# Hybrid attention and mLSTM trunk on one core: f32r scores of split keys and queries, queries moved among the value products, gated outputs a head sooner, roots by Ln and Exp

## The chip, the cores and the metric

One NeuronCore of a Trainium2 chip runs the whole program, with no other core at work. The metric is the device time of one execution in microseconds, as the median over runs. All times in the text are microseconds unless another unit stands beside them.

## What the kernel computes

The reference is a causal trunk of two layers over 512 tokens of 1024 features. Each layer is a half-step SwiGLU FFN, a token mixer and a second half-step FFN. The first layer mixes by dilated attention and pooling; the second by an mLSTM block. The change sits almost wholly in the mLSTM block, cut here to what matters (four heads of 512 channels, `x_c` the convolved tokens, `x_m` the unconvolved ones):

```python
x_m, z = split(xn @ w_in)
x_c = silu(conv(x_m) + conv_b)
q, k, v = blockdiag(x_c, wq), blockdiag(x_c, wk), blockdiag(x_m, wv)   # blocks of 4 channels
...
s_qk = einsum('bhte,bhse->bhts', q, k) * exp(dm - m_t)                 # causal
num, den = s_qk @ v, sum(s_qk)
hh = rms_norm(num / max(abs(den), exp(-m_t)), out_gain)
y = (hh + skip * x_c) * silu(z)
return y @ w_out
```

The kernel does not step through chunks; it takes all 512 tokens of a head at once. The norms before every FFN and mixer are `x * rsqrt(mean(x*x) + 1e-6)`.

## The kernel before

The order of work is written out by hand: each engine has its own list of instructions, and semaphores join them. Data lie features in front of tokens. Most products are taken in float32r, as three products of operands split into a high part (a copy rounded to float32r, written by ScalarE) and a low part (operand less high part, written by VectorE): high by high, low by high, high by low. A few small products are taken in plain float32.

The mLSTM block of `odd_mixer` first runs the input projection, then the four heads, then the output projection (`Q_OOUT`). One head h, on TensorE, before the change:

- **A** (`joined`): the product of the block-diagonal query and key weights, four 128x128 tiles in plain float32. Its input BD is built by GpSimd (`block_diagonals`), and ScalarE copies its result to AM.
- **q0 to q3** (`query`): AM by `x_c`, 512 wide, plain float32; ScalarE copies each to Q.
- **v0 to v3** (`value`): plain float32; ScalarE makes VH of each, then VectorE makes VL.
- **M, EM** (`row`): rows broadcast over the partitions, f32r.
- **mean square** (`mean_square(h - 1)`): sums over the channels the squares of the head before.
- **s0 to s3** (`score`): keys by queries for key block j, 512, 384, 256 and 128 tokens wide, four plain float32 products each.
- **products** j = 0 to 3: the weighted scores by the values, into banks 0 to 3, and the denominator into bank 4. Split on both sides: 12 f32r products and 2 for the denominator each.

A, q, v, M, EM and s are "items". Items go round three PSUM banks (5, 6, 7) in the order of TensorE's list, so item r has to wait until item r - 3 has been read:

```python
if r >= 3:
    pe.wait_ge(item_read[r % 3], r // 3)
return PS[5 + r % 3]
```

What is read: q by ScalarE (L1411), v by ScalarE (VH, L1469) and then VectorE (VL, L2108), s by VectorE (`weighted`, L2118). The chain from a score to the products is: ScalarE takes the weight by Exp (`weight`, L1474), GpSimd cuts it to the causal part (`causal`, L2327), VectorE multiplies the score in (`weighted`), ScalarE takes the high part PTH (`product_high`, L1479), VectorE the low part PTL (`weighted_low`, L2122), TensorE multiplies by the values.

The output of a head runs behind, during the next heads: four squares of the numerator on ScalarE (L1459), which read banks 0 to 3 after the last product; their three sums on VectorE (`squares`, L2073), where the fourth square waits for the first sum since it reuses SQX; the mean square on TensorE; `head_factor` on VectorE; the square root on ScalarE (L1452); its reciprocal on VectorE (`invert_factor`, L2091); `scale_numerator` and `add_skip` on VectorE; `gated` (times silu(z)) on GpSimd; YH on ScalarE and YL (`y_low`, L2322) on GpSimd. The gated outputs of head h - 2 are made during head h.

The ring of four slots that holds the projections' weights (raw, then high and low part) has free places during the heads: slot 3 holds VL, and slots 0 to 2 receive the first three weight tiles of the output projection.

## Time and profile before

| what | value |
|---|---|
| median of 3 runs | 1954.96 us (1954.4 to 1955.63) |
| the profiled execution's own time | 1955.77 us |
| its span in the trace | 1954.0 us |
| PE busy, share of the span | 100% |
| DVE, ACT, POOL busy | 72%, 44%, 27% |
| TensorE's granted clock | 9 (of tenths) in all 40 slices |
| the four heads, first query to the output projection | 1411.66 to 1517.98 us |

The profile is of one execution. A row of a timeline gives the start, the time taken, the engine, the source line and the operation, and behind it in brackets the engine's idle time before it and who ended it. PE's rows overlap, because matmuls are pipelined: what a matmul costs TensorE is the distance from its start to the start of the next, and not the time in its row. A plain float32 matmul leaves two records, so a row of 8 of them is four matmuls.

### The profile page before, as it was taken

Reading aid. Unit: us, or ns where it says so; the run is one execution under the profiler, and the core shown is the slowest. Engines: PE = TensorE matmul, PEld = TensorE weight load, DVE = VectorE, ACT = ScalarE, POOL = GpSimd, SP = SyncE. Lnnn points to the kernel's source line nnn. Section 1 sums busy time; section 2 is a strip of 40 time slices with the busy share of each in tenths; the row PEclk is TensorE's granted clock in tenths of the full one; section 3 lists DMA queues with packets and bytes.
Section 4 is the critical chain, followed back from the end, with each engine's and each line's share of the span. In section 5 each row is a group of like instructions: output and inputs, shape, how many; then the busy total and the mean of one; then the engine's idle time right before and its main releaser. Section 6 shows DMA issues by size and latency. Waiting matters only on the chain.

```text
span 1954.0 us, 28996 instructions
## 1 busy us (share of the span) xinstructions
PE 1948.1 (100%) x11722; PEld 1707.3 (87%) x11722; DVE 1397.9 (72%) x1882; ACT 851.6 (44%) x1230; POOL 527.3 (27%) x394
## 2 busy tenths in 40 slices
PE   9999999999999999999999999999999999999999
PEld 7999998877789999988999998877777888999997
DVE  7877776554588877768877776773458657877773
ACT  6443333535554344345433444442546345333431
POOL 1322222142223322223322322200015413322221
PEclk9999999999999999999999999999999999999999
DMA  6556663351346666545666653232200235666653
GB/s 211 155 164 171 173 168 95 119 181 55 88 126 176 174 172 167 147 129 145 178 166 172 181 151 114 97 96 88 76 1 1 87 116 160 177 173 168 178 141 107
DMA packets 112469, 265.92 MB, mean 136 GB/s; under 512 B 10321, under 2 KB 22865, under 8 KB 112337
## 3 DMA queue, kind: packets, MB, share of 16 engines
q1 hardware_dynamic: 92336, 225.72, 35.3%
q0 software_dynamic: 19856, 38.28, 12.5%
q8 instruction: 93, 1.52, 0.3%
q14 instruction: 40, 0.32, 0.0%
q10 hardware_dynamic: 144, 0.09, 0.0%
HBM read 259.32 MB, written 4.72 MB: 135 GB/s over the span
## 4 chain that ended last, share of the span: by engine, by line
PE 98%; DVE 1%; DMA 0%; issue 0%; ACT 0%; SPq 0%; POOL 0%; DVEq 0%
PE BANKS L656 12%; PE BANKS L658 12%; PE BANKS L657 12%; PE BANKS L579 11%; PE BANKS L580 11%; PE BANKS L581 11%; PE BANKS L709 6%; PE BANKS L710 6%; PE BANKS L711 6%; PE BANKS L1022 2%; PE BANKS L850 1%; PE BANKS L852 1%; PE BANKS L851 1%; PE BANKS L999 1%; PE BANKS L1005 1%; PE BANKS L813 1%
## 5 line engine op out<-in xcount | busy, mean ns | idle before, releaser
L656 PE MATMUL BANKS<-BF,ASH 128*128 128x256 f32 x876 | 248.0, 283 | 0.0
L658 PE MATMUL BANKS<-BF,ASL 128*128 128x256 f32 x876 | 247.9, 283 | 0.0
L657 PE MATMUL BANKS<-BFL,ASH 128*128 128x256 f32 x876 | 247.9, 283 | 0.0
L579 PE MATMUL BANKS<-XH,HI 128*128 128x512 f32 x624 | 245.7, 394 | 0.7 <-DVE XL L1593 0.3
L1657 DVE TENSOR_TENSOR LO<-RING,HI 128x1024 fp32r<-128x1024 f32 (+2 forms) x204 | 216.3, 1060 | 41.2 <-ACT HI L1160 39.9
L580 PE MATMUL BANKS<-XL,HI 128*128 128x512 f32 x624 | 243.2, 390 | 0.0
L581 PE MATMUL BANKS<-XH,LO 128*128 128x512 f32 x624 | 243.0, 389 | 0.0
L1173 ACT ACTIVATE TMP<-TMP 128x512 f32<-128x512 f32 x88 | 55.7, 633 | 406.4 <-DVE TMP L1686 406.4
L2262 POOL TENSOR_TENSOR TMP<-TMP,RSTD 128x512 f32<-128x512 f32 x88 | 132.0, 1499 | 365.3 <-ACT TMP L1173 365.3
L2254 POOL DMA_DIRECT2D ASR<-gu_dram x73 | 88.1, 1219 | 387.5 <-DMA ASR<-gu_dram 381.5
L709 PE MATMUL BANKS<-HH,DHI 128*128 128x512 f32 x488 | 190.7, 391 | 0.0
L710 PE MATMUL BANKS<-HL,DHI 128*128 128x512 f32 x488 | 190.6, 391 | 0.0
L1160 ACT ACTIVATE HI<-RING 128x1024 fp32r<-128x1024 f32 (+2 forms) x204 | 171.4, 876 | 42.3 <-DMA RING<-down_dram 21.4
L711 PE MATMUL BANKS<-HH,DLO 128*128 128x512 f32 x488 | 189.8, 389 | 0.0
L1676 DVE TENSOR_TENSOR ASL<-ASR,ASH 128x1024 fp32r<-128x1024 f32 x146 | 181.6, 1246 | 0.0
L2264 POOL TENSOR_TENSOR HL<-TMP,HH 128x512 fp32r<-128x512 f32 x88 | 139.0, 1580 | 146.6 <-ACT HH L1179 146.6
L1584 DVE TENSOR_TENSOR LO<-RING,HI 128x1024 fp32r<-128x1024 f32 x66 | 85.3, 1294 | 121.6 <-ACT HI L1102 121.5
L656 PEld LDWEIGHTS BANKS<-BF,ASH 128*128 128x128 f32 x876 | 168.2, 192 | 0.0
L657 PEld LDWEIGHTS BANKS<-BFL,ASH 128*128 128x128 f32 x876 | 168.2, 192 | 0.0
L658 PEld LDWEIGHTS BANKS<-BF,ASL 128*128 128x128 f32 x876 | 168.2, 192 | 0.0
L658 PE MATMUL BANKS<-XH,LO 128*128 128x256 f32 x584 | 165.3, 283 | 0.0
L657 PE MATMUL BANKS<-XL,HI 128*128 128x256 f32 x584 | 165.2, 283 | 0.0
(249 smaller groups left out, 4875.5 us busy)
## 6 DMA issues: line engine op xcount, KB each, us to landing
RING<-gu_dram SPq DMA_DIRECT2D x174, 512.0 KB, 3.9
ASR<-gu_dram SPq DMA_DIRECT2D x146, 256.0 KB, 2.9
ASR<-gu_dram POOLq DMA_DIRECT2D x73, 512.0 KB, 6.9
DRAW<-down_dram SPq DMA_DIRECT2D x40, 512.0 KB, 3.7
RING<-oin_dram SPq DMA_DIRECT2D x32, 512.0 KB, 3.5
RING<-down_dram SPq DMA_DIRECT2D x32, 384.0 KB, 3.2
DRAW<-down_dram SPq DMA_DIRECT2D x24, 384.0 KB, 3.7
RING<-ein_dram SPq DMA_DIRECT2D x16, 512.0 KB, 3.6
```

The lines of the kernel that those rows point to most:

```text
L579: pe.matmul(PS[bank][:], HI[j][:, c], hi(k), start=(n == 0), stop=False)
L580: pe.matmul(PS[bank][:], HI[j][:, c], lo(k), start=False, stop=False)
L581: last = pe.matmul(PS[bank][:], LO[j][:, c], hi(k), start=False, stop=(n == len(order) - 1))
L656: pe.matmul(out, w_hi[:, c], x_hi(k), start=(k == 0), stop=False)
L657: pe.matmul(out, w_hi[:, c], x_lo(k), start=False, stop=False)
L658: last = pe.matmul(out, w_lo[:, c], x_hi(k), start=False, stop=(k == 3))
L709: pe.matmul(bank, DHI[:, col], HH[:, h % 8, :], start=(k == 0), stop=False)
L710: pe.matmul(bank, DHI[:, col], HL[:, h % 8, :], start=False, stop=False)
L711: last = pe.matmul(bank, DLO[:, col], HH[:, h % 8, :], start=False, stop=(h == tiles[-1]))
L1160: act.activation(HI[j][:, cols], RAW[j][:, cols], ACT.Copy).then_inc(hi_ready, 1)
L1657: dve.tensor_tensor(LO[j][:, cols], RAW[j][:, cols], HI[j][:, cols].bitcast(F32), ALU.subtract).then_inc(lo_ready, 1)
L1676: dve.tensor_tensor(ASL[:, p % 2, 2 * i:2 * i + 2, :], ASR[:, p % 2, 2 * i:2 * i + 2, :], ASH[:, p % 2, 2 * i:2 * i + 2, :].bitcast(F32), ...
```

## The change

Four things are done, in one diff.

1. **Scores.** ScalarE makes the high part of the keys (XCH, two instructions of 1024 columns a head) and of each query (QH), VectorE the low parts (XCL, QL), and the scores are twelve f32r products a key block where there were four plain float32 ones. Each query item is now read twice, by ScalarE and then by VectorE. XCH, XCL and QL lie in ring slots 0, 1 and 2, so the output projection's first three weight tiles are loaded only when the last score of the last head is done.
2. **Queries.** For heads 1 to 3 the item A stands after the products of j = 0 of the head before (it stood after j = 1), q0 and q1 after those of j = 1, and q2 and q3 after those of j = 2.
3. **Gated outputs.** `gated`, YH and YL of head h - 1 are made during head h, behind the block diagonals on GpSimd.
4. **Roots.** In `norm` and in `root`, Sqrt on ScalarE and reciprocal on VectorE become Ln and Exp (scale -0.5) on ScalarE. TensorE waits for the finished root where it waited for the Sqrt.

The diff, cut to its core:

```diff
 def head_order(h):
-    start = [("q", 0), ("q", 1), ("v", 0), ("q", 2), ("q", 3), ("M", 0), ("v", 1)]
...
-        middle = [("EM", 0), ("v", 2), ("s", 0), ("v", 3), ("s", 1)]
...
+        order = [("v", 0), ("M", 0), ("v", 1), ("v", 2), ("EM", 0), ("s", 0), ("v", 3), ("s", 1)]
...
+            items += [(h + 1, "A", 0)] + [(h + 1, "q", c) for c in range(HT_)]
...
+                    elif q0 == Q_OIN:
+                        sp.wait_ge(item_done, ITEM[(HC - 1, "s", TT - 1)] + 1)
...
                     for c in range(HT_):
-                        last = pe.matmul(ps[:, 0:T - P * j], XC[:, HT_ * h + c, j * P:j * P + P], Q[:, c, j * P:],
-                                         start=(c == 0), stop=(c == HT_ - 1))
+                        pe.matmul(out, XCH[:, c, keys], QH[:, c, j * P:], start=(c == 0), stop=False)
+                        pe.matmul(out, XCH[:, c, keys], QL[:, c, j * P:], start=False, stop=False)
+                        last = pe.matmul(out, XCL[:, c, keys], QH[:, c, j * P:], start=False, stop=(c == HT_ - 1))
...
-                        if j == 1 and h + 1 < HC:
+                        if j == 0 and h + 1 < HC:
                             joined(h + 1)
+                        elif j < TT - 1 and h + 1 < HC:
+                            if j == 1:
+                                read_out(pe, (h + 1, "A", 0))
+                            query(h + 1, 2 * j - 2)
+                            query(h + 1, 2 * j - 1)
...
-                act.activation(RSTD[:], AUX[:], ACT.Sqrt, scale=1.0 / DM, bias=EPST[:]).then_inc(std_ready, 1)
+                link(act.activation(RSTD[:], AUX[:], ACT.Ln, scale=1.0 / DM, bias=EPST[:]))
+                act.activation(RSTD[:], RSTD[:], ACT.Exp, scale=-0.5).then_inc(rstd_ready, 1)
...
+                    if h + 1 < HC:
+                        keys_high(h + 1)
+                        query_high(h + 1, 0)
+                        query_high(h + 1, 1)
+                        y_high(h - 1, 0)
+                        y_high(h - 1, 1)
+                        query_high(h + 1, 2)
+                        y_high(h - 1, 2)
+                        query_high(h + 1, 3)
+                        y_high(h - 1, 3)
+                    else:
+                        split_hi(Q_OOUT, 0, 8)
+                        split_hi(Q_OOUT, 1, 8)
+                        y_high(h - 1, 0)
+                        y_high(h - 1, 1)
+                        split_hi(Q_OOUT, 2, 8)
...
-                dve.wait_ge(std_ready, r + 1)
-                dve.reciprocal(RSTD[:], RSTD[:]).then_inc(rstd_ready, 1)
...
+                def next_head(h):
+                    if h < HC:
+                        keys_low(h, 0)
+                        query_low(h, 0)
+                        query_low(h, 1)
+                        keys_low(h, 2)
+                        query_low(h, 2)
+                        query_low(h, 3)
+                    else:
+                        for j in range(3):
+                            split_lo(Q_OOUT, j, 8)
```

How the instructions stand, at the three places that count. On TensorE, from the last product of a head (L1060, the denominator's last row) to the first score of the next (L1022; names: XC is `x_c`, XM is `x_m`, SELR with MEM are the rows M and EM, SQ the mean square), before:

```order
L1060 MATMUL BANKS<-PTL,SELR 128x128
L999 MATMUL BANKS<-XC,AM 128x512 x2
L1005 MATMUL BANKS<-BD,XM 128x128 x4
L999 MATMUL BANKS<-XC,AM 128x512 x2
L1014 MATMUL BANKS<-MEM,SELR 128x512
L1005 MATMUL BANKS<-BD,XM 128x128 x4
L994 MATMUL BANKS<-SQ,CST 128x512
L1014 MATMUL BANKS<-MEM,SELR 128x512
L1005 MATMUL BANKS<-BD,XM 128x128 x4
```

and the same place of the changed kernel, whose line for the last product is L1070:

```order
L1070 MATMUL BANKS<-PTL,SELR 128x128
L1011 MATMUL BANKS<-BD,XM 128x128 x4
L1020 MATMUL BANKS<-MEM,SELR 128x512
L1011 MATMUL BANKS<-BD,XM 128x128 x8
L1000 MATMUL BANKS<-SQ,CST 128x512
L1020 MATMUL BANKS<-MEM,SELR 128x512
```

The four queries are gone from here, and v1 and v2 follow each other directly ahead of the mean square.

On ScalarE, from the four squares (L1459) to the first two weights (L1474), before:

```order
L1459 ACTIVATE SQX<-BANKS 128x512
L1411 ACTIVATE Q<-BANKS 128x512 x2
L1469 ACTIVATE VH<-BANKS 128x512
L1464 ACTIVATE RSTD<-BANKS 128x512
L1411 ACTIVATE Q<-BANKS 128x512 x2
L1411 ACTIVATE TMP<-BANKS 128x512
L1469 ACTIVATE VH<-BANKS 128x512
L1452 ACT_TABLE_LOAD
L1452 ACTIVATE RSTD<-RSTD 128x512
```

and after the change, with the squares at L1491, VH at L1501 and the root at L1483 and L1484:

```order
L1491 ACTIVATE SQX<-BANKS 128x512
L1501 ACTIVATE VH<-BANKS 128x512
L1496 ACTIVATE RSTD<-BANKS 128x512
L1427 ACTIVATE TMP<-BANKS 128x512
L1501 ACTIVATE VH<-BANKS 128x512 x2
L1483 ACT_TABLE_LOAD
L1483 ACTIVATE RSTD<-RSTD 128x512
L1484 ACT_TABLE_LOAD
L1484 ACTIVATE RSTD<-RSTD 128x512
L1506 ACTIVATE TMP<-TMP,ACOL 128x512
```

VH of v0 stands directly behind the squares, VH of v2 ahead of the root, and the root is two activations with two table loads.

On GpSimd, a head that has an earlier head's output to make, before (L2327 is `causal`, L2317 `gated`, L2322 `y_low`, L2308 the block diagonals):

```order
L2317 TENSOR_TENSOR TMP<-TMP,SZ 128x512 x4
L2327 AFFINE_SELECT TMP<-TMP 128x128
L2322 TENSOR_TENSOR YL<-TMP,YH 128x512
L2327 AFFINE_SELECT TMP<-TMP 128x128
L2322 TENSOR_TENSOR YL<-TMP,YH 128x512
L2327 AFFINE_SELECT WT_96<-WT_96 128x128
L2322 TENSOR_TENSOR YL<-TMP,YH 128x512
L2327 AFFINE_SELECT TMP<-TMP 128x128
L2322 TENSOR_TENSOR YL<-TMP,YH 128x512
L2308 TENSOR_TENSOR BD<-W,CST 128x512 x3
```

and after:

```order
L2398 AFFINE_SELECT TMP<-TMP 128x128 x2
L2398 AFFINE_SELECT WT_99<-WT_99 128x128
L2398 AFFINE_SELECT TMP<-TMP 128x128
L2381 TENSOR_TENSOR BD<-W,CST 128x512 x3
L2388 TENSOR_TENSOR TMP<-TMP,SZ 128x512 x4
L2393 TENSOR_TENSOR YL<-TMP,YH 128x512 x4
```

The eight output instructions moved behind the block diagonals, in one piece.

## Rows read from the trace of the kernel before

**Rows 1.** The page: span, parts 1 and 4

```profile
span 1954.0 us, 28996 instructions
...
PE 98%; DVE 1%; DMA 0%; issue 0%; ACT 0%; SPq 0%; POOL 0%; DVEq 0%
```

**Rows 2.** Waits of TensorE: engine, line waited for: us, times, longest

```profile
PE BANKS L1022 <- DVE VL L2108: 0.4, 1, 0.4
```

**Rows 3.** Timeline of PE, third head: start us, us, engine, line, operation

```profile
1463.26 0.28 PE L1059 MATMUL BANKS<-PTH,SELR 128*128 128x256 f32 x1
1463.38 0.28 PE L1060 MATMUL BANKS<-PTL,SELR 128*128 128x256 f32 x1
...
1464.89 0.27 PE L1060 MATMUL BANKS<-PTL,SELR 128*128 128x128 f32 x1
1465.01 1.93 PE L999 MATMUL BANKS<-XC,AM 128*128 128x512 f32 x4
...
1470.54 1.02 PE L994 MATMUL BANKS<-SQ,CST 128*128 128x512 f32 x2
...
1471.63 1.05 PE L1005 MATMUL BANKS<-BD,XM 128*128 128x128 f32 x8
1472.52 3.60 PE L1022 MATMUL BANKS<-Q,XC 128*128 128x512 f32 x8
...
1476.85 5.36 PE L1022 MATMUL BANKS<-Q,XC 128*128 128x384 f32 x24
1481.96 0.47 PE L1052 MATMUL BANKS<-PTH,VH 128*128 128x512 f32 x1
1482.28 0.39 PE L1053 MATMUL BANKS<-PTL,VH 128*128 128x512 f32 x1
1482.50 0.40 PE L1054 MATMUL BANKS<-PTH,VL 128*128 128x512 f32 x1
```

**Rows 4.** Timeline of ACT, third head

```profile
1463.98 0.60 ACT L1459 ACTIVATE SQ<-BANKS 128x512 f32<-128x512 f32 x1 [1.34 <-PE BANKS L1054]
...
1465.88 0.60 ACT L1459 ACTIVATE SQX<-BANKS 128x512 f32<-128x512 f32 x1 [0.33 <-DVE SQ L2073]
...
1471.41 1.28 ACT L1452 ACT_TABLE_LOAD   x1
1472.82 0.63 ACT L1452 ACTIVATE RSTD<-RSTD 128x512 f32<-128x512 f32 x1
```

**Rows 5.** Timeline of DVE, third head

```profile
1466.69 0.69 DVE L2073 TENSOR_TENSOR SQ<-SQ,SQX 128x512 f32<-128x512 f32 x1
1468.57 0.69 DVE L2108 TENSOR_TENSOR VL<-BANKS,VH 128x512 fp32r<-128x512 f32 x1 [1.19 <-ACT VH L1469]
...
1474.65 3.34 DVE L2091 RECIPROCAL RSTD<-RSTD 128x512 f32<-128x512 f32 x1
...
1479.89 1.72 DVE L2122 TENSOR_TENSOR PTL<-TMP,PTH 128x512 fp32r<-128x512 f32 x1
```

**Rows 6.** Timeline of POOL, third head

```profile
1479.80 1.27 POOL L2322 TENSOR_TENSOR YL<-TMP,YH 128x512 fp32r<-128x512 f32 x1
1481.02 0.75 POOL L2327 TENSOR_SCALAR_AFFINE_SELECT TMP<-TMP 128x128 f32<-128x128 f32 x1
...
1482.98 3.90 POOL L2308 TENSOR_TENSOR BD<-W,CST 128x512 f32<-128x512 f32 x3
```

**Rows 7.** Groups of DVE by line and form: the norms' reciprocals

```profile
L1610 DVE RECIPROCAL RSTD<-RSTD 128x512 f32<-128x512 f32 x6 | 20.1, 3350 | 17.4 <-ACT RSTD L1123 17.4
```

**Rows 8.** Timeline of PE at the end of the heads

```profile
1517.98 0.45 PE L579 MATMUL BANKS<-YH,HI 128*128 128x512 f32 x1
```

**Rows 9.** Timeline of DVE at the end of the heads

```profile
1519.67 0.69 DVE L2073 TENSOR_TENSOR SQ<-SQ,SQX 128x512 f32<-128x512 f32 x1
```

**Rows 10.** The page, part 6: the projection's weights

```profile
RING<-oin_dram SPq DMA_DIRECT2D x32, 512.0 KB, 3.5
```

More of the change, by code:

```diff
@@ L132, in head_order @@
 def head_order(h):
-    start = [("q", 0), ("q", 1), ("v", 0), ("q", 2), ("q", 3), ("M", 0), ("v", 1)]
     if h == 0:
-        middle = [("v", 2), ("v", 3), ("EM", 0), ("s", 0), ("s", 1)]
-    else:
-        middle = [("EM", 0), ("v", 2), ("s", 0), ("v", 3), ("s", 1)]
-    return start + middle + [("s", 2), ("s", 3)]
+        order = [("q", 0), ("q", 1), ("v", 0), ("q", 2), ("q", 3), ("M", 0), ("v", 1), ("v", 2), ("v", 3), ("EM", 0),
+                 ("s", 0), ("s", 1)]
+    else:
+        order = [("v", 0), ("M", 0), ("v", 1), ("v", 2), ("EM", 0), ("s", 0), ("v", 3), ("s", 1)]
+    return order + [("s", 2), ("s", 3)]
 def core_items():
@@ L149, in core_items @@
         if h + 1 < HC:
-            items.append((h + 1, "A", 0))
+            items += [(h + 1, "A", 0)] + [(h + 1, "q", c) for c in range(HT_)]
     return {item: r for r, item in enumerate(items)}
@@ L1413, in read, with keys_high, query_high @@
                     return r
+                def keys_high(h):
+                    if h:
+                        act.wait_ge(item_done, ITEM[(h - 1, "s", TT - 1)] + 1)
+                    for n in range(0, HT_, 2):
+                        act.activation(XCH[:, n:n + 2, :], XC[:, HT_ * h + n:HT_ * h + n + 2, :],
+                                       ACT.Copy).then_inc(xch_ready, 1)
+                def query_high(h, c):
+                    r = ITEM[(h, "q", c)]
+                    act.wait_ge(item_done, r + 1)
+                    act.activation(QH[:, c, :], PS[5 + r % 3][:], ACT.Copy).then_inc(qh_ready, 1)
                 for lq in range(8):
@@ L1451, in root @@
                         act.wait_ge(factor_ready, h + 1)
-                        act.activation(RSTD[:], RSTD[:], ACT.Sqrt).then_inc(tstd_ready, 1)
+                        link(act.activation(RSTD[:], RSTD[:], ACT.Ln))
+                        act.activation(RSTD[:], RSTD[:], ACT.Exp, scale=-0.5).then_inc(factor_root, 1)
                 def square_numerator(h, c):
@@ L1483, in odd_mixer @@
                         square_numerator(h - 1, c)
-                    read(h, "q", 0, Q[:, 0, :])
-                    read(h, "q", 1, Q[:, 1, :])
-                    value_high(h, 0)
-                    denominator(h - 1)
-                    read(h, "q", 2, Q[:, 2, :])
-                    read(h, "q", 3, Q[:, 3, :])
-                    if h:
+                    if h == 0:
+                        query_high(h, 0)
+                        query_high(h, 1)
+                        value_high(h, 0)
+                        query_high(h, 2)
+                        query_high(h, 3)
+                    else:
+                        value_high(h, 0)
+                        denominator(h - 1)
                         read(h, "M", 0, TMP[:, 6, :])
@@ L1493, in odd_mixer @@
                     value_high(h, 1)
-                    root(h - 1)
                     value_high(h, 2)
@@ L2087, in head_factor, with root_ready @@
                                              ALU.add).then_inc(factor_ready, 1)
[L2089 to L2091 removed]
+                def root_ready(h):
+                    dve.wait_ge(factor_root, h + 1)
                 def scale_numerator(h, c):
@@ L2109, in value_low, with query_low @@
                                       ALU.subtract).then_inc(read, 1)
+                def query_low(h, c):
+                    ps, read = item(h, "q", c)
+                    dve.wait_ge(qh_ready, HT_ * h + c + 1)
+                    dve.tensor_tensor(QL[:, c, :], ps[:], QH[:, c, :].bitcast(F32), ALU.subtract).then_inc(read, 1)
                 def row_copy(h, name, n):
@@ L2123, in weighted_low @@
                                       ALU.subtract).then_inc(ptl_ready, 1)
+                def next_head(h):
[6 more added lines that the diff above has]
+                        query_low(h, 3)
+                    else:
+                        for j in range(3):
+                            split_lo(Q_OOUT, j, 8)
+                query_low(0, 0)
+                query_low(0, 1)
                 value_low(0, 0)
+                query_low(0, 2)
+                query_low(0, 3)
                 row_copy(0, "M", 6)
@@ L2156, in odd_mixer @@
                     weighted_low(h, 2)
+                    weighted(h, 3)
                     add_skip(h - 1, 2)
-                    weighted(h, 3)
                     weighted_low(h, 3)
                     add_skip(h - 1, 3)
+                    next_head(h + 1)
                 squares(HC - 1)
@@ L2349, in _ @@
             for h in range(HC):
-                for c in range(HT_ if h >= 2 else 0):
-                    gated(h - 2, c)
                 for j in range(TT):
                     causal(h, j)
-                    if h >= 2:
-                        y_low(h - 2, j)
                 if h + 1 < HC:
                     block_diagonals(h + 1)
-            for h in (HC - 2, HC - 1):
-                for c in range(HT_):
-                    gated(h, c)
-                for c in range(HT_):
-                    y_low(h, c)
+                for c in range(HT_ if h else 0):
+                    gated(h - 1, c)
+                for c in range(HT_ if h else 0):
+                    y_low(h - 1, c)
+            for c in range(HT_):
+                gated(HC - 1, c)
+            for c in range(HT_):
+                y_low(HC - 1, c)
             for m in range(KX):
```

72 lines of the change are left out of this document (40 added, 32 removed).

## The prediction

> **What bounds the kernel now.** I read the page first: TensorE is busy for the whole span and holds 98% of the chain that ended last [rows 1]. Busy matmul records overlap, so that alone could hide waiting; the view of TensorE's waits says that it does not: in the heads the only one listed is 0.4 at the first score [rows 2]. Then I took the timeline of TensorE in the third head and read distances from start to start. The heads run at the pace of TensorE's own list. So work taken off that list is worth its full time, and a new wait costs its full time. The timelines of the other three engines in the same head [rows 4 to 6] say how near they are to being late; that is what decides here.
>
> **What TensorE saves.** Before, s0 costs 1476.85 - 1472.52 less v3 in between (1472.52 - 1471.63 = 0.89), so 3.44; s1 to s3 end where the first product starts, 1481.96 - 1476.85 = 5.11; together 8.55 a head [rows 3]. An f32r matmul costs 0.22 at 512 columns (1482.28 to 1482.50), 0.12 at 256 (1463.26 to 1463.38) and 0.12 at 128 (1464.89 to 1465.01) [rows 3]; 384 is not in the rows and I take 0.17 between them. Twelve of each: 12 x 0.63 = 7.56. The saving is 1.0 a head, 3.9 in all with rounding. It comes from the wide blocks; at 128 columns three products cost more than the plain one.
>
> An f32r matmul that follows a plain one takes 0.1 longer (1481.96 to 1482.28 is 0.32 [rows 3]). Queries between the products and v3 between s0 and s1 make such changes: counted over the lists, one more in head 0, two more in heads 1 and 2, none in head 3, so 5 x 0.1 = 0.5. **TensorE: -3.4.**
>
> **The wait at v2.** v2 takes the bank of v0, so it needs VL of v0. Let E be the end of a head's products, 1465.01 in the rows. The squares start at E - 1.03 and the fourth at E + 0.87, since it waits for the first sum [rows 4]; the third sum starts at E + 1.68 and runs 0.69 [rows 5], and VL of v0 stands behind it. Before, four queries (a quarter of s0 each, 0.86, so 3.4) lay between E and the value items, and VL of v0 at 1468.57 [rows 5] was early. Those queries now lie ahead of E. TensorE wants v2 at E + v0 0.89 + M 0.32 + v1 0.89 = E + 2.1; VL can start at E + 2.35 and is read through at E + 3.0, or 3.1 with the handover. That is 1.0 in each of heads 1 to 3, whatever else happens.
>
> In heads 2 and 3 two things add to it. ScalarE has the last QH and the last YH ahead of the squares: the last query ends the 14 x 0.12 of j = 3 before E, at E - 1.7, and two activations of 0.6 with a handover of 0.2 bring the first square to E - 0.3, 0.7 later than before. And GpSimd is then in the middle of four y_low. What that does is in the rows: a PTL of 512 columns took 1.72 on VectorE where other instructions of that size took 0.69, over a y_low that had begun at 1479.80 and takes 1.27, and the next GpSimd instruction, a select of a quarter of that width, took 0.75 [rows 5, 6]. VectorE waited for the end of GpSimd's instruction and GpSimd then for VectorE's. Each of the three sums can meet one, 0 to 1.2 lost on the chain; I take 0.9. So 2.6 a head, from 1.0 to 3.2. **v2: 1.0 + 2 x 2.6 = +6.2.**
>
> The Trainium skill (SBUF — State Buffer, "SBUF: two separate sides") states that VectorE and GpSimd share a port pair by an exclusive lock, held for a whole instruction, for VectorE instructions with two SBUF inputs against a GpSimd one that reads SBUF. The rows agree with it for PTL; by it the sum is my forecast, and without it the first rival's.
>
> **The wait at A.** A now stands behind j = 0 and still needs the block diagonals. Let m be the start of the mean square, 1470.54 [rows 3]. Before, the block diagonals end at 1482.98 + 3.90 = m + 16.3 [rows 6], and A came behind j = 1, about m + 17.4 (1481.96 + 14 x 0.22 + 14 x 0.17 + 0.1). The margin was 1.0. Now TensorE wants A at: mean square and EM 1.09, s0 12 x 0.22 = 2.7, v3 0.89, s1 to s3 12 x 0.41 + 0.1 = 5.0, j = 0 3.1; so m + 12.8, 4.6 sooner. GpSimd's chain: `head_factor` is now behind VL of v2 (v2 ends at m; 0.6, 0.69 and handovers, m + 1.5), done at m + 2.2; Ln 0.63 (as Sqrt), table load 1.28, Exp 0.63 [rows 4], m + 4.8; then on VectorE scale 0, weighted 0, scale 1, VL of v3, PTL 0, scale 2, weighted 1, seven at 0.6, m + 9.0; PTH 1, weight 3 and causal 3, which stand in one chain now, 1.5, m + 10.5; block diagonals 3.4 to 3.9, m + 13.9 to m + 14.4. VectorE's `add_skip` reads two SBUF operands and runs at the same time; one exchange as above adds 1.1. The root itself is sooner (before, the reciprocal ended at 1474.65 + 3.34 = m + 7.45 [rows 5]), and that is why the miss is no larger. The wait is 1.1 to 2.7 and I take 2.4. It falls in heads 1 and 2; in head 0 nothing is behind. **A: +4.8.**
>
> Here the Trainium skill (ScalarE: Activation LUTs, "What ACT_TABLE_LOAD costs") speaks against the new roots: a change of set costs 2.66 with a drain. In the trace the load begins at 1471.41 and the Sqrt at 1472.82, 1.41 later with its wait in it [rows 4], so the drain is not seen, and the sum goes by 1.28.
>
> **Head 0.** q2 takes q0's bank, now read by ScalarE (0.6) and then VectorE (0.69), while ScalarE still has the last z tile; v1 waits for q2 likewise. No row has it; 0.2 to 1.4, and I take **+1.0**.
>
> **The end.** T is the end of all products, 1517.98 [rows 8]. Before, the third sum ended at 1519.67 + 0.69 = T + 2.4 [rows 9], and the mean square behind 24 matmuls of 0.22 was due at T + 5.4. Now VectorE has three low parts of weight tiles first. Their loads start after the last score, which ends 14 x 0.63 = 8.8 before T. One tile takes 3.5 [rows 10], three of them 3.5 to 10.5, so the third lands between T - 5.3 and T + 1.7; near the middle, T - 0.3. High and low part at about 1.2 each (estimate: twice the columns of the 0.69), the low part ends at T + 2.2, the sums at 0.8 each at T + 4.6. But `gated` and y_low of head 2 now run just here, and four VectorE instructions may meet one each, up to T + 9.1. So 0 to 3.7, and I take **+2.4**. The first two weight tiles are there in time: T - 5.3 plus 2.4 for the first.
>
> **Costed at nothing.** Six norms lose 3.35 each on VectorE [rows 7] and gain 1.9 each on ScalarE (a table load and an Exp). TensorE waits at none of them now [rows 2], so the earlier root gains nothing, and its own wait for the root comes 6 or more tiles of 5.4, over 30, behind the norm, against 3.8 for the root. Without that cover it would be up to 1.9 each. The splits of keys and the query halves run while TensorE is on products; the scores need them 8 later.
>
> **Sum.** -3.4 + 6.2 + 4.8 + 1.0 + 2.4 = +11.0. On the profiled execution's 1955.8 that is 1966.8; the median of the runs stands 0.8 lower: **1966**. With all lower ends: -3.4 + 0.2 + 3.0 + 2.2 + 0 = +2.0, so 1957; with all upper ends -3.4 + 1.4 + 7.4 + 5.4 + 3.7 = +14.5, so 1969.5.
>
> **Rivals.**
> - *GpSimd and VectorE hardly meet.* For it: they meet only if instructions happen to overlap. Against: four `gated` and four y_low in one piece. v2 1.0 + 2 x 1.7, A 2 x 1.3, head 0 1.0, the end 0.3: +4.9, so **1960**.
> - *The waits stay covered, faster.* It decides at VL of v0: if it is read by E + 2.1, and the block diagonals are done by m + 12.8. Then -3.4, the 0.5 for changes of kind may hide as well, and the 0.4 that the first score waits now [rows 2] may go, so -4.3: **1950.7**. Against it, the chain of three sums is fixed in length by rows 4 and 5.
> - *A table change drains ScalarE first.* 1.4 more on the root's chain, so 2.8 more at the two A: **1969**. The rule above from the page on ScalarE gives this.
> - *The ring.* If the three loads come one after the other in full, low parts 2.0 later and tile 1 late too: 1968 to 1972.
>
> **Chances.** Forecast (1962 to 1968) 0.5; few meetings (1957 to 1962) 0.2; table drain 0.06; ring or more of the same 0.12; waits partly covered, within 0.2% (about 3.9, which is what a measurement of this kernel can tell) 0.06; faster 0.06. Range 1957 to 1971.
>
> **What would show it.** Scores of 7.6 a head; a wait of 1.0 before v2 in head 1, and more in heads 2 and 3, ended by VL; a wait before A in heads 1 and 2, ended by GpSimd's BD, and none in head 0; sums of over 1 where GpSimd runs y_low; the last mean square later than T + 5.4. I am wrong if ScalarE reads v0 ahead of the squares in effect, if the block diagonals finish by m + 12.8, or if a norm's longer root is met by TensorE.

## The result and the profile after

The changed kernel takes 1972.09 us (median of 4 runs, 1969.66 to 1972.54) against 1954.97 (4 runs, 1954.4 to 1955.63): a ratio of 1.0084, 95% interval 1.0071 to 1.0097. It is slower, as forecast, but by 17 where 11 was the sum, and 1.1 above the upper end of the range.

The page of the profiled execution of after: the span, TensorE's busy time and the chain that ended last.

```profile
span 1970.8 us, 29183 instructions
...
PE 1951.4 (99%) x11786; PEld 1719.2 (87%) x11786; DVE 1398.6 (71%) x1896; ACT 876.6 (44%) x1257; POOL 537.4 (27%) x394
...
PE 95%; DVE 2%; ACT 1%; issue 1%; DMA 0%; POOL 0%; DVEq 0%; POOLq 0%
```

The span grew by 16.8 (from 1954.0). TensorE holds 95% of the chain where it held 98%, and VectorE 2% where it held 1% [rows 1]. The view of TensorE's waits, after, from 1405 to 1560 (engine, line waited for: us in total, times, longest), says at which items:

```profile
PE BANKS L1011 <- DVE VL L2158: 6.9, 3, 3.2
PE BANKS L1000 <- DVE SQ L2124: 3.6, 1, 3.6
PE BANKS L965 <- POOL BD L2381: 2.8, 2, 2.1
PE BANKS L1011 <- DVE QL L2164: 0.4, 1, 0.4
PE BANKS L1030 <- DVE VL L2158: 0.2, 1, 0.2
PE BANKS L1005 <- DVE QL L2164: 0.2, 1, 0.2
```

Before there was one row in this stretch, of 0.4 [rows 2]. L1011 is a value item, L1000 the mean square, L965 is A. These rows leave out handovers (the time from the end of the work waited for to TensorE's start); the sizes below are distances from start to start, less what the matmuls in front take at their pace. Now TensorE's timeline at the end of the third head's products and up to the first score, the stretch that answers to [rows 3]:

```profile
1502.67 0.27 PE L1070 MATMUL BANKS<-PTL,SELR 128*128 128x128 f32 x1
1502.79 1.10 PE L1011 MATMUL BANKS<-BD,XM 128*128 128x128 f32 x8
1503.64 0.47 PE L1020 MATMUL BANKS<-MEM,SELR 128*128 128x512 f32 x1
1503.96 1.05 PE L1011 MATMUL BANKS<-BD,XM 128*128 128x128 f32 x8
1508.22 2.08 PE L1011 MATMUL BANKS<-BD,XM 128*128 128x128 f32 x8 [3.21 <-DVE VL L2158]
1510.10 1.78 PE L1000 MATMUL BANKS<-SQ,CST 128*128 128x512 f32 x2
1511.02 1.08 PE L1020 MATMUL BANKS<-MEM,SELR 128*128 128x512 f32 x1
1511.94 0.40 PE L1030 MATMUL BANKS<-QH,XCH 128*128 128x512 f32 x1
```

v0 and v1 cost 0.86 each. v2 waits 3.4, and then it costs 1.88, twice as much, for the same eight records. The mean square and EM behind it take 1.84, where they took 1.09 before (1470.54 to 1471.63 [rows 3]). From v2 to the first score it is 3.72; in head 1 of after, behind a wait of 1.2, it is 2.08 (1443.81 to 1445.89). That is 1.6 more, over and above the wait. The windows of after say why; the columns are the stretch, its length, the busy time of PE, PEld, DVE, ACT and POOL with the number of records, then the granted clock of TensorE as a share of full, the DMA share and GB/s:

```profile
1456.00:1460.00 4.00, 1.95 (x9) 1.28 (x8) 4.00 (x6) 0.42 (x1) 4.00 (x4) 1.00 0.00 0
1460.00:1464.00 4.00, 4.00 (x18) 4.00 (x19) 2.04 (x3) 2.53 (x4) 4.00 (x3) 0.57 0.00 2
1472.00:1476.00 4.00, 1.69 (x15) 1.46 (x13) 3.37 (x4) 3.49 (x7) 2.39 (x2) 1.00 0.01 2
1476.00:1480.00 4.00, 3.61 (x13) 2.39 (x14) 3.60 (x7) 1.93 (x3) 0.00 (x0) 0.69 0.01 4
1504.00:1508.00 4.00, 1.01 (x9) 0.82 (x7) 3.79 (x4) 2.86 (x6) 2.22 (x2) 1.00 0.00 0
1508.00:1512.00 4.00, 3.77 (x12) 2.79 (x13) 2.76 (x6) 1.64 (x2) 0.00 (x0) 0.57 0.01 2
1534.00:1538.00 4.00, 0.96 (x5) 0.45 (x3) 3.79 (x3) 2.37 (x3) 3.91 (x3) 1.00 0.43 130
1538.00:1542.00 4.00, 3.40 (x7) 2.11 (x8) 3.04 (x5) 0.80 (x2) 0.00 (x0) 0.61 0.00 1
```

Four times the clock falls to its lower level (1.2 GHz) when TensorE comes back from a wait, or up to 1.1 later: A in head 1, v2 in head 2, v2 in head 3, and the last mean square. Twice the missing share of a window is the time at half clock: 2 x 0.43 x 4.00 = 3.4 behind A and behind v2 in head 3. Before, the clock was full in the heads. Each fall costs 1.6 (1.58 to 1.64 against the same stretch at full clock), so 6.5 in all. The fall at A shows as 5.02 from A to the first query (1459.85 to 1464.87), and 3.44 one head later at full clock. This term stands nowhere in the prediction.

The sum of after against before, from the distances in the trace:

| term | predicted | measured |
|---|---|---|
| scores and changes of kind | -3.4 | -3.9: 7.64 for 8.62 in head 0, 8.46 for 9.44 with v3 in head 1; nothing lost by changes of kind |
| v2, heads 1, 2, 3 | 1.0 + 2.6 + 2.6 | 1.2 + 2.9 + 3.4 |
| A, heads 1, 2 | 2.4 + 2.4 | 2.2 + 0.9 |
| head 0, first query to first score | 1.0 | 1.0 (9.19 for 8.17) |
| last mean square | 2.4 | 3.8 |
| half clock behind waits | none | 6.5 |
| before the heads | 0 | -1.1 |
| sum | +11.0 | +16.9 (span: +16.8) |

Differences of 0.2 and less are left out, among them 0.2 less at the first products of heads 2 and 3. The -1.1 is no effect of the change that I can show: the first query starts at 1410.52, before at 1411.66. In three kernels below whose instructions up to there are those of before (e10, e11, e12) it starts at 1411.52, 1411.01 and 1411.17, and in those that share them with after (e2 to e9) between 1410.33 and 1411.17.

### The profile page after: what moved, and what is told of

It is laid out like the page before. It is cut to its first block, busy times and chain, and to the rows that moved or that the text cites. A ratio compares the mean times of both kernels' runs of the same rounds, so it can differ in the third digit from the quotient of the medians.

```text
span 1970.8 us, 29183 instructions
## 1 busy us (share of the span) xinstructions
PE 1951.4 (99%) x11786; PEld 1719.2 (87%) x11786; DVE 1398.6 (71%) x1896; ACT 876.6 (44%) x1257; POOL 537.4 (27%) x394
## 3 DMA queue, kind: packets, MB, share of 16 engines
q0 software_dynamic: 19856, 38.28, 12.6%
## 4 chain that ended last, share of the span: by engine, by line
PE 95%; DVE 2%; ACT 1%; issue 1%; DMA 0%; POOL 0%; DVEq 0%; POOLq 0%
PE BANKS L662 12%; PE BANKS L664 12%; PE BANKS L663 12%; PE BANKS L585 11%; PE BANKS L586 11%; PE BANKS L587 11%; PE BANKS L715 6%; PE BANKS L716 6%; PE BANKS L717 6%; PE BANKS L856 1%; PE BANKS L858 1%; PE BANKS L857 1%; DVE SQ L2124 1%; PE BANKS L819 1%; PE BANKS L919 1%
## 5 line engine op out<-in xcount | busy, mean ns | idle before, releaser
L585 PE MATMUL BANKS<-XH,HI 128*128 128x512 f32 x624 | 245.5, 393 | 0.5 <-DVE LO L2271 0.2
L2327 POOL DMA_DIRECT2D ASR<-gu_dram x73 | 88.1, 1226 | 390.3 <-DMA ASR<-gu_dram 384.5
```

What stands on the lines that cost most here:

```text
L585: pe.matmul(PS[bank][:], HI[j][:, c], hi(k), start=(n == 0), stop=False)
```

## Why the waits are as long as they are

What VectorE, ScalarE and GpSimd did at the same place of after, in their timelines:

```profile
1502.62 0.60 ACT L1491 ACTIVATE SQ<-BANKS 128x512 f32<-128x512 f32 x1
...
1505.20 0.60 ACT L1491 ACTIVATE SQX<-BANKS 128x512 f32<-128x512 f32 x1 [1.00 <-DVE SQ L2124]
1505.69 0.59 ACT L1501 ACTIVATE VH<-BANKS 128x512 fp32r<-128x512 f32 x1
...
1503.74 1.36 DVE L2124 TENSOR_TENSOR SQ<-SQ,SQX 128x512 f32<-128x512 f32 x1 [0.73 <-ACT SQX L1491]
1505.21 1.56 DVE L2124 TENSOR_TENSOR SQ<-SQ,SQY 128x512 f32<-128x512 f32 x1
1506.88 0.69 DVE L2124 TENSOR_TENSOR SQ<-SQ,SQX 128x512 f32<-128x512 f32 x1
1507.49 0.68 DVE L2158 TENSOR_TENSOR VL<-BANKS,VH 128x512 fp32r<-128x512 f32 x1
...
1499.73 6.50 POOL L2393 TENSOR_TENSOR YL<-TMP,YH 128x512 fp32r<-128x512 f32 x4
```

Four y_low take 6.50, to 1506.23. The first two sums lie over them and take 1.36 and 1.56; the third starts after and takes 0.69, what it took before [rows 5]. VL of v0 ends at 1508.17, and v2 starts at 1508.22. ScalarE has a share too: in this head the first square starts 0.17 before the end of the products (1502.62 for 1502.79), in head 1 0.82 before it (1439.75 for 1440.57), because the high parts YH now stand ahead of the squares. The same at the end, from the last low parts of weights to the last sum:

```profile
1527.73 5.68 DVE L1629 TENSOR_TENSOR LO<-RING,HI 128x1024 fp32r<-128x1024 f32 x3
1533.34 1.78 DVE L2124 TENSOR_TENSOR SQ<-SQ,SQX 128x512 f32<-128x512 f32 x1
1535.22 1.57 DVE L2124 TENSOR_TENSOR SQ<-SQ,SQY 128x512 f32<-128x512 f32 x1
1536.89 1.57 DVE L2124 TENSOR_TENSOR SQ<-SQ,SQX 128x512 f32<-128x512 f32 x1
...
1530.06 7.85 POOL L2393 TENSOR_TENSOR YL<-TMP,YH 128x512 fp32r<-128x512 f32 x4
...
1527.89 1.06 ACT L1117 ACTIVATE HI<-RING 128x1024 fp32r<-128x1024 f32 x1 [0.22 <-DMA RING<-oout_dram]
```

The third tile's high part starts at 1527.89, 1.4 before the end T of the products at 1529.27, so the loads were in time, even 1.1 sooner than assumed. The low parts took 1.9 each (assumed: 1.2), the sums 1.6 to 1.8 (assumed: 0.8): all six lay over GpSimd's work, the first low part over the last `gated`, the others over y_low. The last sum ends at T + 9.2, near the T + 9.1 that the prediction gave as the worst case, and the mean square starts at 1538.60 in place of T + 5.5.

The root on ScalarE, behind `head_factor`:

```profile
1512.71 0.63 ACT L1483 ACTIVATE RSTD<-RSTD 128x512 f32<-128x512 f32 x1 [0.48 <-DVE RSTD L2137]
1513.36 1.28 ACT L1484 ACT_TABLE_LOAD   x1
1514.66 0.63 ACT L1484 ACTIVATE RSTD<-RSTD 128x512 f32<-128x512 f32 x1
```

From the start of Ln to the end of Exp it is 2.58, and the table load takes 1.28 with nothing beside it. The Trainium skill (ScalarE: Activation LUTs, "What ACT_TABLE_LOAD costs") would have put a drain on top; the trace does not agree, and the measurement decides.

## The experiments

What had to be told apart: whether the excess is the half clock behind the waits (the clock theory), or the waits' own length, by y_low and the sums getting into each other's way (the meetings), or the new roots. Times of all kernels, each with the kernel before run beside it:

| kernel | median us (range, runs) | ratio to before, 95% |
|---|---|---|
| e1 before, new roots alone | 1955.29 (1954.72 to 1955.92, 11) | 1.0000 (0.9991 to 1.0009) |
| e2 after, two waits filled | 1969.79 (1969.22 to 1971.0, 5) | 1.0076 (1.0063 to 1.0090) |
| e3 after, v0 first | 1970.23 (1969.11 to 1970.39, 4) | 1.0075 (1.0060 to 1.0090) |
| e4 after, diagonals first | 1967.37 (1965.22 to 1968.32, 4) | 1.0061 (1.0046 to 1.0076) |
| e5 e3, e4 and a later mean square | 1963.46 (1962.66 to 1964.64, 4) | 1.0044 (1.0027 to 1.0060) |
| e6 after, gated outputs late again | 1973.6 (1973.17 to 1975.01, 4) | 1.0098 (1.0082 to 1.0115) |
| e7 after, old root in the heads | 1975.9 (1975.37 to 1977.02, 4) | 1.0109 (1.0092 to 1.0126) |
| e8 e6, v0 and diagonals first | 1973.16 (1972.64 to 1973.72, 4) | 1.0093 (1.0077 to 1.0110) |
| e9 e3, e4 and y_low moved | 1958.51 (1958.3 to 1958.88, 10) | 1.0016 (1.0007 to 1.0026) |
| e10 before, a wait put in | 1960.08 (1957.64 to 1961.98, 11) | 1.0023 (1.0014 to 1.0032) |
| e11 e10, the wait filled | 1958.45 (1957.84 to 1959.39, 11) | 1.0017 (1.0008 to 1.0026) |
| e12 before, queries moved alone | 1960.69 (1959.83 to 1961.01, 7) | 1.0027 (1.0016 to 1.0038) |

**e1: part 4 alone, on the kernel before.** The same pair of activations in `root`.

```diff
-                act.activation(RSTD[:], AUX[:], ACT.Sqrt, scale=1.0 / DM, bias=EPST[:]).then_inc(std_ready, 1)
+                link(act.activation(RSTD[:], AUX[:], ACT.Ln, scale=1.0 / DM, bias=EPST[:]))
+                act.activation(RSTD[:], RSTD[:], ACT.Exp, scale=-0.5).then_inc(rstd_ready, 1)
```

> The kernel before with part 4 of the change alone: Ln and Exp for Sqrt and reciprocal, in the norms and in the heads. Theory (nothing of the extra time is in the roots): TensorE waits nowhere new, 1955 within 1, and the heads take 106.3 as before. Rival (the norms' longer root is met by TensorE, or three more table loads cost): 1.9 for each norm met, so 1957 to 1966.

No change, and TensorE's only wait in the heads is the old 0.4. The six norms and the roots of the heads were rightly costed at nothing on the kernel before; whether they are part of the excess of after, the next run says.

**e7: the opposite, the old root in the heads of after.** With e1 it shows whether the new root helps once the block diagonals are wanted sooner.

```diff
-                        link(act.activation(RSTD[:], RSTD[:], ACT.Ln))
-                        act.activation(RSTD[:], RSTD[:], ACT.Exp, scale=-0.5).then_inc(factor_root, 1)
+                        act.activation(RSTD[:], RSTD[:], ACT.Sqrt).then_inc(factor_root, 1)
...
+                    link(dve.reciprocal(RSTD[:], RSTD[:]))
```

> The changed kernel with Sqrt and reciprocal again in the heads, the norms left as changed. Theory (the new roots are a help: the root is on the chain to the fourth weight and so to the block diagonals): root ready 2.6 later, A waits 2 to 2.6 longer in heads 1 and 2, one more clock drop: 1976 to 1979. Rival (Ln and Exp with their table loads on ScalarE are part of the loss): 1970 or less.

3.8 slower than after, though the clock falls three times and not four. A waits 2.4 in both heads, the third score 0.8 in head 1 and 0.5 in head 2, and v2 3.4 in heads 2 and 3. So the new root is worth 3.8 here and nothing in the kernel before: it is no part of the excess, and it pays only where another engine waits for it.

**e2: two waits of after filled with work that nobody needs.** Eight f32r matmuls ahead of A's wait in head 1, sixteen ahead of the last mean square; their result is overwritten.

```diff
+                    for _ in range(8 if h == 2 else 0):
+                        pe.matmul(ps[:], SELR[:, HC:HC + 1].to_broadcast([P, P]), PTH[:, 0:T], start=True, stop=True)
                     pe.wait_ge(bd_ready, h + 1)
...
+                                pe.wait_ge(bank_free, 4 * Q_OOUT + 2)
+                                for _ in range(16):
+                                    pe.matmul(PS[7][:], SELR[:, HC:HC + 1].to_broadcast([P, P]), PTH[:, 0:T],
+                                              start=True, stop=True)
                                 mean_square(HC - 1)
```

> The changed kernel with matmuls that do nothing useful put into two of TensorE's long waits: 8 f32r products of 512 columns ahead of the wait for the block diagonals in head 1, and 16 behind the first output tile, ahead of the last mean square. They write banks that are overwritten afterwards, so the result is the same. Theory (the waits of 2 and more drop TensorE's granted clock to half, and each drop costs about 1.7 on top of the wait): the two stretches at half clock behind these waits are gone, and with 24 more matmuls the kernel is 3.4 faster, about 1968.7. Rival (the excess is only longer waiting, and the clock falls along with it without a cost of its own): no faster than 1972, or slower by what the added matmuls overhang.

With 24 more matmuls the profiled span is 3.1 shorter (1967.7) and the median 2.3; the runs of the two kernels overlap (1969.22 to 1971.0, and 1969.66 to 1972.54 for after), so this pair alone would be thin. The trace is clearer. Three of the four falls are gone, two of them at the filled waits; the third, at v2 in head 2, had nothing filled, and its wait is still 3.4 long. So a wait of this size makes the clock fall in some cases and not in others. Three falls less are 4.9; A in head 2 (2.3 for 0.9) and v2 in head 2 (3.4 for 2.9) take 1.9 of it back, which leaves 3.0. The waits at v2 and at A in head 2, e2:

```profile
1475.40 1.16 PE L1013 MATMUL BANKS<-BD,XM 128*128 128x128 f32 x8 [3.25 <-DVE VL L2164]
...
1491.53 1.13 PE L967 MATMUL BANKS<-BD 128*128 128x128 f32 x8 [2.13 <-POOL BD L2387]
```

They also say why A in head 2 waits only 0.9 in after. v2 waits as long here, and A waits 2.3 behind it; what is missing is the fall between them. In after TensorE lost 1.6 at half clock behind the mean square while GpSimd's chain ran on, and so came to A that much later.

**e10 and e11: the same question on the kernel before.** e10 makes TensorE wait for an event 3.3 late ahead of the last mean square; e11 puts 14 useless matmuls ahead of that wait.

```diff
                             if first and j == 0:
+                                pe.wait_ge(bank_free, 4 * Q_OOUT + 2)
+                                for _ in range(14):
+                                    pe.matmul(PS[7][:], SELR[:, HC:HC + 1].to_broadcast([P, P]), PTH[:, 0:T],
+                                              start=True, stop=True)
+                                pe.wait_ge(y_ready, 4 * (HC - 1))
                                 mean_square(HC - 1)
```

(e10 is the same with the line on `y_ready` alone.)

> The kernel before with one wait and nothing else: TensorE takes the last mean square only when the gated outputs of head 2 are all made, which comes 3.3 after the end of the first output tile. Theory (a long wait costs itself and then a stretch at half the clock): 1955 + 3.3 + 1.7 = 1960, in those executions in which the clock falls, 1958.3 in the others. Rival (a wait costs itself): 1958.3.

> The same wait in the kernel before, with 14 f32r matmuls of 512 columns (3.2) ahead of it, which write a bank that the next tile overwrites. Both theories: 1958.3 in every execution, and the granted clock stays full. The difference to the run without the matmuls is the price of the clock: 1.7 by the one theory, 0 by the other.

The windows of e10, the wait in the first:

```profile
1522.00:1526.00 4.00, 1.50 (x7) 0.92 (x5) 0.00 (x0) 2.46 (x3) 4.00 (x4) 0.96 0.34 99
1526.00:1530.00 4.00, 3.38 (x6) 2.06 (x7) 1.19 (x2) 0.55 (x2) 3.00 (x3) 0.50 0.08 32
1530.00:1534.00 4.00, 4.00 (x14) 3.13 (x13) 3.86 (x3) 3.10 (x5) 2.54 (x2) 0.69 0.01 4
```

and of e11:

```profile
1522.00:1526.00 4.00, 4.00 (x19) 3.19 (x17) 0.00 (x0) 2.55 (x3) 4.00 (x4) 1.00 0.42 128
1526.00:1530.00 4.00, 4.00 (x17) 2.76 (x16) 2.39 (x3) 1.76 (x4) 3.22 (x4) 1.00 0.01 3
```

Both do the same useful work and release at the same event, 8.8 (e10) and 8.9 (e11) behind the end of the products, where before needs 5.5. In the profiled executions e10 is 6.0 over before's span (1960.0) and e11 2.9 (1956.9). From the mean square to the twentieth row behind it TensorE takes 8.06 in e10 (1526.62 to 1534.68) and 5.30 in e11 (1526.27 to 1531.57): the wait is worth 3.3, and the half clock behind it 2.8 more. Over the runs the medians are 1.6 apart, because e10 varies: of its 11 runs the two with the full mean clock took 1957.64 and 1958.37, the seven at 0.999 1959.29 to 1960.53, the two at 0.998 1961.73 and 1961.98. e11 was at full clock in all. That settles the clock theory: the wait is the same, the time goes with the mean clock, and filling the wait removes both.

**e3: v0 of the value items read ahead of the fourth square (ScalarE) and of the second and third sums (VectorE).**

```diff
-                    for c in range(HT_):
+                    for c in range(HT_ - 1):
                         square_numerator(h - 1, c)
+                    if h:
+                        value_high(h, 0)
+                    square_numerator(h - 1, HT_ - 1)
...
-                    squares(h - 1)
+                    squares(h - 1, (0,))
                     value_low(h, 0)
+                    squares(h - 1, (1, 2))
```

> The changed kernel with VH of v0 ahead of the fourth square on ScalarE and VL of v0 ahead of the second and third sum on VectorE, in heads 1 to 3. Theory (v2 waits for VL of v0, which stands behind three sums that meet GpSimd's y_low): the wait before v2 falls from 1.2, 2.9 and 3.4 to 0.2 to 1.2 each, some 5 in all, and two of the four drops of the clock go with it, 3.4; part comes back as the mean square then waits for the sums, up to 1 a head. 1964 to 1967. Rival (v2 is only where TensorE notices a late VectorE, which then makes the mean square just as late): 1971 or more.

The waits at v2 shrink to 0.5 to 0.9, but 0.5 to 1.0 comes at the mean square and 0.8 at the first score. A waits 2.1 in head 1 and 2.1 in head 2 as well, where no fall of the clock stands ahead of it any more, and the last mean square 4.0. It missed its expectation by 3: VectorE's chain only changed which item waits for it. There is one fall of the clock for four, but it lasts 6.8 where each had lasted 3.4.

**e4: the block diagonals ahead of the fourth causal cut on GpSimd.**

```diff
                 for j in range(TT):
+                    if j == TT - 1 and h + 1 < HC:
+                        block_diagonals(h + 1)
                     causal(h, j)
-                if h + 1 < HC:
-                    block_diagonals(h + 1)
```

> The changed kernel with the block diagonals ahead of the fourth causal cut on GpSimd. Theory (A waits for the block diagonals, which stand behind a chain through the fourth weight): the wait of 2.2 in head 1 and 0.9 in head 2 are gone, with one drop of the clock, so 3.1 + 1.7 = 4.8 less, about 1967. Rival (the fourth weighted score becomes late instead and TensorE waits at the products of j = 3): 1970 or more.

Both waits at A are gone, which confirms that the fourth cut held GpSimd back. v2 keeps 1.2, 3.7 and 2.9, and the last mean square 4.0. The span fell by 5.6 (1965.2): 3.1 of wait, and two falls of the clock for four. The wait of 2.9, at v2 in head 3, brought none.

**e5: e3 and e4 together, and the last mean square a tile later.** Its edit beside theirs:

```diff
-                            if first and j == 0:
+                            if first and j == 1:
                                 mean_square(HC - 1)
```

> The changed kernel with v0 read first, the block diagonals ahead of the fourth causal cut, and the last mean square behind the second output tile. Theory (three waits and the clock that falls with them are the whole excess): of v2's wait 0.9 and of the mean square's and the first score's 1.0 each stay in each of heads 1 to 3, no clock drop is left, so 1955 - 3.4 - 1.1 for an earlier start + 0.9 in head 0 + 3 x 2.9 = 1960. Rival (more of the excess sits where it has not been looked for, or the waits pass on to the products): 1964 or more.

It missed its 1960 by 3.5. The wait at the last mean square went, and 2.1 came back at the output projection's next tile behind it (L585). Two falls of the clock are left, one with no wait over 1.5 shortly ahead of it: v2 waits 0.7 there and the mean square 1.4.

**e6: part 3 undone.** `gated`, YH and y_low of head h - 2 run during head h again.

```diff
             for h in range(HC):
+                for c in range(HT_ if h >= 2 else 0):
+                    gated(h - 2, c)
                 for j in range(TT):
                     causal(h, j)
+                    if h >= 2:
+                        y_low(h - 2, j)
                 if h + 1 < HC:
                     block_diagonals(h + 1)
-                for c in range(HT_ if h else 0):
-                    gated(h - 1, c)
-                for c in range(HT_ if h else 0):
-                    y_low(h - 1, c)
```

> The changed kernel with part 3 undone: gated outputs of head h - 2 during head h, as before. Theory (half of v2's wait in heads 2 and 3, and most of the wait of the last mean square, come from VectorE's sums meeting y_low on GpSimd): v2 waits 1.2 in all three heads, the last mean square at most 0.5, three of the four clock drops go; A waits 1 to 2 more in head 2, since four y_low are then ahead of the block diagonals: 1972 - 3.9 - 3.6 - 5 + 2 = 1961. Rival (v2 waits for the squares' order alone and the last mean square for the ring's weights): v2 still near 3 in heads 2 and 3, 1970 or more.

Here the theory of meetings is put to the proof: all twelve sums take 0.69, v2 waits 1.2 in each of the three heads, and the wait at the last mean square is gone. But e6 undoes two things at once, since the high parts YH leave their place ahead of the squares as well: in e6 the first square starts 0.82 before the end of the products in each of these heads, and in heads 2 and 3 of after 0.15 and 0.17 before it. So of the 1.7 and 2.2 over 1.2, the later squares are 0.7 and 0.65, and the meetings the rest: 1.0 (sums of 0.84 and 1.57) and 1.5 (1.36 and 1.56). The rule of the Trainium skill (SBUF — State Buffer, "SBUF: two separate sides"), that one of the two engines then holds the port pair for a whole instruction, agrees: of the seven sums that lay over a y_low in after, six took 0.7 to 1.1 more and one 0.15 more, and no sum did here. Yet the time is 1.5 worse than after and 12.6 over the theory, since new waits stand in TensorE's list. The view of its waits, e6:

```profile
PE BANKS L1030 <- DVE TMP L2173: 4.1, 2, 2.1
PE BANKS L1062 <- DVE TMP L2146: 4.0, 2, 2.8
PE BANKS L965 <- POOL BD L2381: 3.6, 2, 2.0
```

and VectorE's row ahead of the first:

```profile
1482.44 0.75 DVE L2146 SCALAR_TENSOR_TENSOR TMP<-BANKS,PAR,RSTD 128x512 f32<-128x512 f32 x1 [4.87 <-POOL YL L2395]
```

The scaled output of head h - 1 goes where y_low of head h - 2 still reads; VectorE stands idle for 4.87, and the weighted score queued behind it, with the next score's bank, is late. The change had also put the first scaling ahead of the first weighted score in VectorE's list (L2146 ahead of L2173), and e6 left that as it is. In e12 below, where the weighted score stands first (at 1479.72, the scaling at 1481.07), the gated outputs are late too, and no score or product waits for VectorE's weighted scores.

**e8: e6 with v0 and the diagonals first.** No new line; the edits of e3 and, after the third cut, e4.

> Parts 1, 2 and 4 of the change with both cures: gated outputs of head h - 2 as before, v0 read first, block diagonals ahead of the fourth causal cut and of the last two y_low. Theory: v2 waits 0.5, the mean square 0.5 and the first score 0.5 in heads 1 to 3, A and the last mean square not at all, no clock drop: 1955 - 3.4 + 0.9 + 4.5 = 1957 at most, 1953 if those three small waits are gone. Rival (the saving of the scores is eaten by waits that come with the moved queries in any order): 1960 or more.

A miss by 16: the waits of e6 at the scores and products stay (2.1 in heads 2 and 3, then 2.7 and 3.2 in head 2), with two long falls of the clock. I had counted only the waits that e3 and e4 cure, not the one that y_low brings.

**e9: e3 and e4, with gated outputs early as in after, but YH and y_low of head h - 2 ahead of the root of head h - 1.** So y_low can neither meet the sums nor hold the scaled output.

```diff
             for h in range(HC):
+                for c in range(HT_ if h >= 2 else 0):
+                    y_low(h - 2, c)
...
-                for c in range(HT_ if h else 0):
-                    y_low(h - 1, c)
+            for c in range(HT_):
+                y_low(HC - 2, c)
```

> The changed kernel with v0 read first, the block diagonals ahead of the fourth causal cut, and YH and y_low of head h - 2 moved to where ScalarE waits for the root of head h - 1, so that y_low no longer runs beside the sums. Theory (y_low beside the sums makes v2 and the mean square late in heads 2 and 3, and the last mean square): in heads 1 to 3 v2, the mean square and the first score wait 0.5, 0.5 and 0.9, as in head 1 of the runs before, A and the last mean square not at all, no clock drop: 1955 - 3.4 + 0.9 + 5.7 = 1958 to 1960. Rival (a new wait at the weighted scores, because the scaling waits for y_low): 1963 or more.

The waits of TensorE, e9:

```profile
PE BANKS L1030 <- DVE VL L2158: 2.0, 4, 0.6
PE BANKS L1011 <- DVE VL L2158: 1.1, 3, 0.4
PE BANKS L1000 <- DVE SQ L2124: 1.0, 3, 0.3
```

and the sums, with the shortest, median and longest in ns:

```profile
L2124 DVE TENSOR_TENSOR SQ<-SQ,SQX x8: 679/692/694, 1440.7 to 1525.2; 128x512 f32<-128x512 f32 x8
```

No sum is long, no wait is over 1, and the clock stays full: 13.6 better than after. It is the best version with all four parts, and still 0.16% slower than before (0.07 to 0.26): the waits of 0.5 at v2, 0.5 at the mean square and some 0.8 at the first score, in each of three heads, outweigh what the scores save. No kernel here beats the one before.

**e12: part 2 alone, on the kernel before.** Plain float32 scores, old roots, old gated outputs.

```diff
-                        if j == 1 and h + 1 < HC:
+                        if j == 0 and h + 1 < HC:
                             joined(h + 1)
+                        elif j < TT - 1 and h + 1 < HC:
+                            if j == 1:
+                                read_out(pe, (h + 1, "A", 0))
+                            query(h + 1, 2 * j - 2)
+                            query(h + 1, 2 * j - 1)
```

> The kernel before with part 2 of the change alone: A behind j = 0 and the queries among the products, plain float32 scores, Sqrt and reciprocal, gated outputs as before. Theory (the wait at v2 comes from the queries' place alone, the one at A from its own): v2 waits 1.2 in each of heads 1 to 3 as in the changed kernel's head 1; A is met later than the block diagonals by 1 to 2 in heads 1 and 2; 1955 + 3.6 + 3 = 1961.5. Rival (the waits need the split of the queries, which has VectorE read them): within 1 of 1955.

The waits of TensorE, e12:

```profile
PE BANKS L1005 <- DVE VL L2120: 3.0, 3, 1.0
PE BANKS L959 <- POOL BD L2320: 1.6, 1, 1.6
```

By distances v2 waits 1.2 in each of three heads and A 1.7 once: 5.3, of the 5.7 by which the stretch from the first query to the output projection grew (112.06 for 106.32). The clock is full throughout. This is the base that the prediction put at 1.0 "whatever else happens", with nothing of parts 1, 3 and 4 in it.

## Why the prediction was off

The direction and the places were right, point by point:

- **What TensorE saves** (-3.4): -3.9. The scores are right, 7.64 a head for 7.56. The 0.5 for changes of kind is not there: v3 between the split scores costs 0.80 where it cost 0.89, and so gives back what the f32r matmul behind it loses.
- **The wait at v2** (+6.2): right in place and cause, 7.5 in size. The base is 1.2 (e12, e6), where the prediction had 1.0; later squares and meetings added 1.7 and 2.2, for 1.6 each.
- **The wait at A** (+4.8): 3.1. In head 1 2.2, near the forecast. In head 2 0.9, because the fall of the clock behind v2 had held TensorE back by 1.6 between the mean square and A; where that fall is missing, it waits 2.3 (e2) and 2.1 (e3). e4 takes both waits away.
- **Head 0** (+1.0): 1.0.
- **The end** (+2.4): 3.8. The loads were in time; the step that failed is "High and low part at about 1.2 each" and "the sums at 0.8 each". The low parts took 1.9 and the sums 1.6 to 1.8: every one of six instructions met GpSimd, where four might.
- **Costed at nothing**: right, by e1. Of the rivals, "GpSimd and VectorE hardly meet" is refuted by the sums of 1.4 to 1.8, "a table change drains ScalarE first" by the trace, and "the ring" by the third tile, read at T - 1.4. "The waits stay covered" fails at VL of v0, 3.3 past its point in head 3.

**The step that failed** is the premise of the first paragraph, "a new wait costs its full time". It costs more than its time: behind four of them the clock fell to half, and that was 6.5. The other terms were off by +1.3 (v2), -1.7 (A), +1.4 (the end), -0.5 (TensorE's own work) and -1.1 (before the heads); that these come to -0.6 together is luck, and it leaves the clock as the whole miss of 6. Its net share is less, 5 by estimate, since some 1.4 was won back at A in head 2 (0.9 for the 2.3 of e2). That the half clock has a price of its own is shown best by e10 and e11 (1.6 between the medians, 2.8 in the pair of traces, and 11 runs in step with the mean clock); e2 points the same way with 2.3 between the medians. The range had no term for it. With it, the forecast's own upper ends would have reached past 1972.

Not settled: which waits bring the fall. One of 3.4 did not in e2, one of 2.9 did not in e4, one of 2.2 did in after, and the same wait in e10 fell differently from run to run.

## What to carry to other kernels

Work that stands between two dependent stretches of TensorE's list is cover for the other engines' chains; moving it into a stretch that has no need of cover saves nothing by itself and uncovers the chain behind (e12: +5.5). Where TensorE is the bound and has no waits, price a new wait of 2 and more as its time and then, perhaps, a stretch at half clock as well: 1.6 each here, and 2.8 in e10. Price each VectorE instruction with two SBUF inputs that lies over a GpSimd one at twice its length (the sums here, six of seven), and look at where a moved block of GpSimd work will come to lie before moving it.

## What the hardware showed beyond that

- Useless matmuls made a kernel faster: 24 of them took 2.3 off the median and 3.1 off the profiled span (e2), with one fall of the granted clock in place of four.
- The half clock lasted 3.4 in each of the four falls of after, and 6.8 in the one of e3, one of two in e6, both of e8 and the one of e10.
- f32r matmuls started 0.227, 0.174, 0.12 and 0.112 apart at 512, 384, 256 and 128 columns, so 128 columns cost nearly what 256 do.
- A low part of a 128x1024 weight tile took 1.9 on VectorE beside GpSimd's gated outputs and y_low (5.68 for three), where one of the keys of that size took 1.22 with GpSimd idle (head 1 of after), and a y_low there 1.96 (7.85 for four) where one had taken 1.27 [rows 6].
